# Sink attention in a two-block model: other banks for the second rotation, a new order on three engines, and an earlier fetch of the distance table

## What is computed

```python
def banded_sink_attention(q, k, v, sinks):
    logits = jnp.einsum('bnqhgd,bnkhd->bnhgqk', qb, kw) * (dh ** -0.5)
    logits = jnp.where(valid, logits, -jnp.inf)  
    m = jnp.maximum(jnp.max(logits, axis=-1), sink)
    probs = jnp.exp(logits - m[..., None])
    denom = jnp.sum(probs, axis=-1) + jnp.exp(sink - m)
    return jnp.einsum('bnhgqk,bnkhd->bnqhgd', probs, vw) / denom[..., None]

def swa_sink_mixer(h, positions, w_qkv, q_norm, k_norm, sinks, w_out):
    q, k, v = jnp.split(h @ w_qkv, [1024, 1280], axis=-1)
    q = apply_rope_2(rms_norm_2(q, q_norm), cos, sin)
    k = apply_rope_2(rms_norm_2(k, k_norm), cos, sin)
    return banded_sink_attention(q, k, v, sinks) @ w_out
```

## Time and profile before

| | |
|---|---|
| median of 3 runs | 2091.65 us (2090.82 to 2091.75) |
| the profiled execution: its own time | 2096.21 us |
| its span, first to last instruction | 2094.3 us |
| granted TensorE clock, mean over the span | 0.995 |
| PE / DVE / ACT / POOL busy | 99% / 85% / 67% / 3% |
| bytes moved, mean rate | 565.92 MB, 270 GB/s |

### The profile page before, as it was taken

The page is one execution under the profiler, slowest core; times in us unless marked ns, Lnnn a source line. Parts: engine busy times, 40 slices in busy tenths (PEclk is TensorE's granted clock), DMA queues, the critical chain, the costliest instruction groups (busy, mean ns, idle before and its releaser), DMA issues. The chain is left out here.

```text
span 2094.3 us, 27806 instructions
## 1 busy us (share of the span) xinstructions
PE 2067.1 (99%) x10830; PEld 1740.9 (83%) x10830; DVE 1779.1 (85%) x2358; ACT 1400.0 (67%) x1855; POOL 59.6 (3%) x58
## 2 busy tenths in 40 slices
PE   9999999999999999999999999999999999999999
PEld 8878888878888888888888888879988888778887
DVE  6776768789999999999999999988878888788887
ACT  5654547568888888888888888867745446565544
POOL 0011002001000000000000000000000000000000
PEclk9999999999999999999999999999999999999999
DMA  9537764659999999999999999954446555346552
GB/s 312 181 121 271 233 209 151 219 199 395 394 395 395 395 395 383 385 380 386 371 393 374 388 372 378 394 202 141 144 159 227 196 181 149 81 154 222 183 197 102
DMA packets 291275, 565.92 MB, mean 270 GB/s; under 512 B 13596, under 2 KB 120224, under 8 KB 290896
## 3 DMA queue, kind: packets, MB, share of 16 engines
q1 hardware_dynamic: 284480, 537.13, 71.8%
q0 software_dynamic: 5792, 23.78, 3.1%
q10 hardware_dynamic: 864, 3.15, 0.4%
HBM read 555.10 MB, written 12.59 MB: 271 GB/s over the span
## 5 line engine op out<-in xcount | busy, mean ns | idle before, releaser
L505 DVE TENSOR_TENSOR wl<-raw,wh 128x1024 fp32r<-128x1024 f32 x626 | 756.2, 1242 | 99.9 <-ACT wh L497 95.5
L497 ACT ACTIVATE wh<-raw 128x1024 fp32r<-128x1024 f32 x626 | 640.9, 1053 | 154.1 <-PE psum L542 61.7
L505 DVE TENSOR_TENSOR wl<-arena,wh 128x1024 fp32r<-128x1024 f32 x384 | 456.7, 1222 | 37.6 <-ACT wh L497 32.6
L497 ACT ACTIVATE wh<-arena 128x1024 fp32r<-128x1024 f32 x384 | 403.9, 1062 | 84.7 <-PE psum L542 82.5
L540 PE MATMUL psum<-wh,xhl 128*128 128x512 f32 (+1 forms) x1136 | 449.5, 396 | 1.8 <-DVE wl L505 0.9
L542 PE MATMUL psum<-wh,xhl 128*128 128x512 f32 (+1 forms) x1136 | 441.5, 389 | 0.0
L541 PE MATMUL psum<-wl,xhl 128*128 128x512 f32 (+1 forms) x1136 | 440.6, 388 | 0.0
L532 PE MATMUL psum<-xhl,wh 128*128 128x512 f32 x980 | 349.4, 396 | 0.0
L540 PE MATMUL psum<-wh,yh 128*128 128x512 f32 x752 | 295.6, 393 | 1.0 <-DVE yl L1714 1.0
L542 PE MATMUL psum<-wh,yl 128*128 128x512 f32 x752 | 293.0, 390 | 0.0
L541 PE MATMUL psum<-wl,yh 128*128 128x512 f32 x752 | 292.6, 389 | 0.0
(11 more groups left out here) (455 smaller groups left out, 2078.1 us busy)
## 6 DMA issues: line engine op xcount, KB each, us to landing
arena<-in_moe_g SPq DMA_DIRECT2D x72, 1024.0 KB, 8.8
arena<-in_moe_u SPq DMA_DIRECT2D x72, 1024.0 KB, 8.5
raw<-in_moe_d SPq DMA_DIRECT2D x64, 1024.0 KB, 8.8
arena<-in_moe_d SPq DMA_DIRECT2D x48, 1024.0 KB, 8.3
raw<-in_ff_up SPq DMA_DIRECT2D x48, 1024.0 KB, 5.2
raw<-in_moe_g SPq DMA_DIRECT2D x40, 1024.0 KB, 8.1
raw<-in_moe_u SPq DMA_DIRECT2D x40, 1024.0 KB, 9.2
raw<-in_ff_down SPq DMA_DIRECT2D x24, 1024.0 KB, 5.4
```

Of the source, the lines that this page charges most:

```text
L497: A.activation(unit_made(s, i)[0], raw_half(s, i), ACT.Copy).then_inc(*s.w_hi.tick(i))
L505: V.tensor_tensor(lo, raw_half(s, i), hi.bitcast(F), SUB).then_inc(*s.w_lo.tick(i))
```

## The change

It does five things:

- the rotation of the second half of the queries goes to banks 2 and 3 in place of 0 and 4;
- on PE `turned(3)` comes ahead of `sums(1)`;
- on DVE the masks of pieces 4 and 6 come ahead of the scales, `rows(0, 1)` too; the maxima of 4 and 6 come in a row, those of 5 and 7 share their three small steps; `rows(1, 0)` and the low parts of U+16 and U+17 move;
- on ACT `newer(5)` comes ahead of `soft(4)` and `newer(7)` ahead of `soft(6)`, and the high parts of some units come later;
- at the beginning the `hold_clock` after the first chunk has 2 matmuls in place of 3, and POOL fetches the distance table without waiting for x.

```diff
-                    hold_clock(7, 3, STILL[:, 0:P], STILL)
+                    hold_clock(7, 2, STILL[:, 0:P], STILL)
...
-    Q_BANKS, RO_BANKS, SS_BANK = {2: (0,), 0: (2, 3), 1: (0, 4)}, {2: (6,), 0: (6, 7), 1: (0, 4)}, {2: 4, 0: 4, 1: 1}
+    Q_BANKS, RO_BANKS, SS_BANK = {2: (0,), 0: (2, 3), 1: (0, 4)}, {2: (6,), 0: (6, 7), 1: (2, 3)}, {2: 4, 0: 4, 1: 1}
...
         logits(4, 6)
+        turned(3)
         sums(1)
-        turned(3)
         weigh(0, 1)
...
         turned(1)
+        turned(3)
         hi_to(main, U + 15)
-        turned(3)
-        hi_to(main, U + 16)
         weighed(0, 1)
         hi_to(main, U + 17)
+        newer(5)
         soft(4)
-        newer(5)
+        newer(7)
+        soft(6)
         hi_to(main, U + 18)
-        soft(6)
-        newer(7)
-        hi_to(main, U + 19)
         soft(5)
         turned(4)
         turned(6)
-        hi_to(main, U + 20)
+        hi_to(main, U + 19)
         soft(7)
         weighed(1, 0)
-        hi_to(main, U + 21)
+        hi_to(main, U + 20)
         turned(5)
         turned(7)
...
-        def maxima(u):
+        def maxima(*us):
...
+            for n, u in enumerate(us):
+                V.wait_ge(*dve.of(f"wi.l{u}"))
+                V.tensor_reduce(x[:, n, :], WE[u % 4], AX, MAX, negate=True).then_inc(*dve.tick())
...
         normal(3)
+        part_older(1)
         rows(0, 0)
-        part_older(1)
+        masked(4)
         part_older(3)
+        masked(6)
+        rows(0, 1)
         scales(1)
-        rows(0, 1)
+        maxima(4)
+        maxima(6)
         lo_to(main, U + 14)
-        begin(4)
+        older(5)
         lo_to(main, U + 15)
-        begin(6)
-        begin(5)
+        older(7)
+        maxima(5, 7)
         lo_to(main, U + 16)
         normal(4, 6)
-        begin(7)
+        lo_to(main, U + 17)
+        normal(5)
+        rows(1, 0)
         lo_to(main, U + 18)
-        normal(5)
         normal(7)
-        rows(1, 0)
...
-        G.wait_ge(*x_in[0].of("all"))
         G.dma_start(CT[0:32, o:o + n], d["consts"][0:32, o:o + n]).then_inc(*distances_in.tick())
```

More of the change, by code:

```diff
@@ L3223, in older, with soft_pair @@
                                   heads(bk(b), 2)[:, :, 0:P]).then_inc(*dve.tick(f"wi.l{u}"))
-        def maxima(u):
-            nm, _, sk, x = soft_cols(u)
-            gr, t, L = u // 2, u % 2, WE[u % 4]
-            _, r, _, _ = win_scales(gr // 2)
-            r4 = r[:, 8 * t:8 * t + 8].rearrange("p (j g) -> p g j", g=2)[:, gr % 2, :]
-            V.wait_ge(*dve.of(f"wi.l{u}"))
-            V.tensor_reduce(x, L, AX, MAX, negate=True).then_inc(*dve.tick())
+        def soft_pair(*us):
+            a = 64 + 16 * us[0]
+            return (SC[:, a:a + 64].rearrange("p (u n j) -> p u n j", u=2, j=4)[:, 0:len(us), n, :] for n in range(4))
+        def maxima(*us):
+            t, gr = us[0] % 2, us[0] // 2
+            _, r, _, _ = win_scales(gr // 2)
+            r4 = r[:, 8 * t:8 * t + 8].rearrange("p (j g) -> p g j", g=2)[:, gr % 2:gr % 2 + len(us), :]
+            ns = NSK[:, 4 * gr:4 * gr + 4 * len(us)].rearrange("p (u j) -> p u j", j=4)
+            nm, _, sk, x = soft_pair(*us)
+            for n, u in enumerate(us):
+                V.wait_ge(*dve.of(f"wi.l{u}"))
+                V.tensor_reduce(x[:, n, :], WE[u % 4], AX, MAX, negate=True).then_inc(*dve.tick())
             V.wait_ge(*dve.last())
@@ L3234, in maxima @@
             V.wait_ge(*dve.last())
-            V.tensor_tensor(nm, x, NSK[:, 4 * gr:4 * gr + 4], MIN).then_inc(*dve.tick())
+            V.tensor_tensor(nm, x, ns, MIN).then_inc(*dve.tick())
             V.wait_ge(*dve.last())
-            V.tensor_tensor(sk, nm, NSK[:, 4 * gr:4 * gr + 4], SUB).then_inc(*dve.tick(f"wi.m{u}"))
+            V.tensor_tensor(sk, nm, ns, SUB).then_inc(*dve.tick(*[f"wi.m{u}" for u in us]))
         def begin(u):
```

## The result

The changed kernel takes 2100.18 us, median of 12 runs (2095.71 to 2104.39). The kernel before, run beside it on the same chip, takes 2093.05 us, also 12 runs (2090.52 to 2097.20). The ratio is 1.0031 with an interval of 1.0020 to 1.0042. The change costs 7.1 us, where I had forecast 2.1. It is slower by 0.3% (the interval begins at 0.2%), and outside my range, also when the range is counted from this 2093.05 in place of the 2091.65 of three runs that I started from: it then ends 5.85 us above before.

The account below looks back on a forecast made before the run. PE was taken as the bound, busy 2067.1 of 2094.3 us. From 2091.65 us, -2.7 (beginning) + 1.6 (attention lists) + 3.2 (clock falls) = +2.1 gave 2093.7 us, range 2087.5 to 2097.5.

Parts of the forecast that it names:

- The lists: Sink attention: new engine orders worked against each other; projection 5.8 us earlier, then new PE waits, feed-forward part 1.6 us later.
- Rival 1: Sink attention: PE keeps the 5.8 us of the earlier projection, 2083.1 us; chance 0.13, another 0.05 for half of it.
- I take two falls, behind the two waits nearest to 3.48: +3.2 us: Sink attention: two of four new PE waits bring half clock, up to 1.6 us each; between 0 and 6.4 us.
- rival 2: Sink attention: the clock falls behind each of the four new waits, 4 x 1.6 us, giving 2097.0 us; chance 0.14.
- the beginning's bound: Kernel start: the small end of the beginning's gain, -1.5 us, if the clock falls there all the same.
- The term of the beginning, -2.7 us: Kernel start: earlier table fetch -1.5, half clock gone -1.6, one `hold_clock` matmul less -0.1, taken back +0.4 and +0.1 us.
- Rival 3: Kernel start: the beginning gives nothing, through a held-up first chunk or a clock falling anyway; 2096.5 us, chance 0.08.
- its first reason: Kernel start: the distance table's early fetch holds up the first chunk.
- the 0.1 us that I had put down for the table: Kernel start: the table's 48.5 KB now move beside the first chunk at 348 GB/s, costing some 0.1 us.

Follow-up runs that it names:

- e4: The whole change, with PE's four new waits in the attention filled by matmuls nobody reads: 2093.94 us, ratio 1.0002 to the kernel before.
- e6: e5 with four matmuls nobody reads added in PE's wait for the rotated queries, ahead of `logits(4, 6)`: 2086.59 us, ratio 0.9967 to before.
- e2: The changed kernel with the two edits of the beginning undone: 2098.58 us, ratio 1.0033 to the kernel before.
- e3: The kernel before with only the second half's rotation moved to banks 2 and 3, all lists as before: 2091.11 us, ratio 0.9990.
- e7: The kernel before with 7 matmuls nobody reads in PE's old 3.48 us wait ahead of the second rotation: 2092.62 us, ratio 0.9997.
- e8: e4 with `scales(1)` back ahead of `rows(0, 1)` on DVE and no filling behind `logits(5)`: 2091.89 us, ratio 0.9993 to before.
- e9: e8 with `normal(7)` ahead of `rows(1, 0)` on DVE and no filling ahead of `turned(7)`: 2091.06 us, ratio 0.9986 to before.
- e10: e9 with pieces 5 and 7 in their old places on ACT and DVE, filling only ahead of `logits(4, 6)`: 2086.76 us, ratio 0.9970 to before.
- e5: The kernel before with the start edits, rotation in banks 2 and 3, and `turned(3)` ahead of `sums(1)`; old DVE and ACT lists: 2089.90 us, ratio 0.9981.
- e1: The kernel before with the two edits of the beginning alone: 2092.47 us, ratio 0.9993.

## Why the prediction was wrong, point by point

**The lists were right.** Each wait came where it was put: ahead of `logits(4, 6)` 1.83 us (2.0 said), behind `logits(5)` for the low part 2.56 (2.8), ahead of `turned(4)` 2.86 (3.1), ahead of `turned(7)` 3.07 (3.3). The projection's start gained 5.9 us (5.8). With no fall in the stage it is 55.76 - 54.47 = 1.3 us longer (e4 against before); 1.6 was said. Rival 1, that the gain of 5.8 us stays, is refuted by the same rows. It does come true, and more, once the lists of DVE and ACT are the old ones and the first wait is filled: e6 has 48.16 us, 6.3 less than before.

**The step that failed** is "I take two falls, behind the two waits nearest to 3.48: +3.2 us". In the profiled execution it is exact: two falls, and the stage is 58.91 - 55.76 = 3.15 us longer than with the waits filled. But the forecast is for the median of many runs, and there the falls cost 6.2 us, the price I gave to rival 2 (6.4) with a chance of 0.14. The mechanism differs from rival 2's in its form, as far as the mean clocks and the profiled e2 tell (no run of the changed kernel's own lower group was profiled): not each wait with one fall of 1.6 us, but half of the runs with few falls, and half with many or long ones, as e2's 10 us in one piece, 20 us in all, worth 63.78 - 55.76 = 8.0 us of the stage. So the mis-sized thing was the cost of one fall: my 1.6 us is half of the 3.3 us at the beginning, where the same rows show 6.8 us in the stage itself, behind a wait followed by light work. The Trainium skill (TensorE: Matmul & The Clock Gate, Part 1) says that the gate does not start anew with a kernel, and that the number of slow matmuls at its start varies from run to run. The runs agree and show it in mid-kernel too: 2095.7 to 2104.4 us for one program at clocks of 0.997 to 0.992, and 2092.4 to 2096.0 with the waits filled. I had kept both ends of the range for this reason, and then put the middle where one execution would lie. Two slips of the working changed nothing in the sum: with the clock falling all the same the beginning's bound is -2.7 + 1.6 = -1.1 and not -1.5, and by my own terms the change costs more than it gives from the first fall on (-1.1 + 1.6 = +0.5), not from the third.

**The term of the beginning, -2.7 us, was mis-sized.** Alone it measured -0.6 by the medians and -1.5 by the ratio (-3.3 to +0.4 by the interval, so 2.7 is not excluded by that run alone); with it undone the rest of the change costs as much as all of it (1.0033 and 1.0031). In the profiled pair it is there in full: the matmuls of L1127 start at 34.9 before and at 31.9 after. But that execution before was an unlucky one: the other three with the old beginning start them at 32.7 (e2), 32.1 (e3) and 32.0 (e7), since the table landed sooner and the clock did not fall. The eight with the new beginning start them at 31.3 to 32.2, 31.7 in the mean. So old and new are 0.6 us apart in the mean, 1.2 with the execution before counted. Rival 3, that the beginning gives nothing, is near in size, though its first reason is not borne out: no hold-up of the first chunk can be told. ACT's first copy waits for that chunk, and starts at 3.55 to 3.73 us in the four executions with the old beginning and at 3.56 to 3.76 in the eight with the new one; the 0.1 us that I had put down for the table beside that chunk is below this scatter.

**The sum with the measured terms**: -0.6 for the beginning, +1.5 for the lists (e4 is 0.9 above before, and the beginning's 0.6 is in it), +6.2 for the clock: +7.1 us. The three add up by construction, since e4 is subtracted in one and added in the other. The +1.5 and the +6.2 hang on the same runs of e4; the stage's 1.3 is an independent reading of the first, and the 6.7 us of lost clock of the second. e2 is the check from outside: 1.5 + 6.2 = 7.7 us without the beginning, where it measured 5.5 by the medians and 6.9 by the ratio. So these terms are good to a us or two.

**Where the gain of the banks went** can be told part by part from the stages without half clock. From e6 to e4 are 7.6 us: the scales behind `rows(0, 1)` cost 2.3 (e4 to e8), `normal(7)` behind `rows(1, 0)` costs 1.0 (e8 to e9), the odd pieces ahead of `normal(4, 6)` cost 3.1 (e9 to e10, on DVE and ACT together). The last 1.2 us, e10 to e6, are the masks ahead of the scales and the units' places, and were not taken apart.

**What stays open.** Why the clock doesn't fall at all in one execution (after, behind the wait of 1.83 us) and falls for 10 us in another (e2, behind the same wait) was seen and not explained. How many of the 6.2 us come from the first wait alone wasn't tried on the changed kernel; e4 fills all four at once.

## What to carry to other kernels

On an engine that works its list in order, a wait costs what stands behind it: all three orders that lost time here put a step that waits for PE (`rows`, `older`) ahead of one that PE waits for (`scales`, `normal`). On a PE that is 99% busy, a wait of 2 us can be followed by more half clock than it is long, so a wait that cannot be removed is worth filling with matmuls: four of them were worth 3.3 us from e5 to e6. Look at the next wait too, since in e7 the fall only moved there and nothing clear was gained (filling both wasn't tried on that kernel). And price no term of a few us from one execution: read it in several, and look at the mean clock of every run before believing the profile's pair.

## What was not expected of the hardware

- The clock falls behind waits much shorter than 3.48 us: 1.82 us in e3, 1.24 us in e7. In both, narrow matmuls follow (64 rows, 128x2); the fall comes during the first of them in e3 and at their end in e7. That they play a part was not tested. In the other direction, waits of 1.83 and 3.07 us after the change were followed by no fall in the profiled execution.
- The falls of this stage lasted about 3.4, 6.8 or 10.2 us, by the execution.
- The same work falls or doesn't by the execution. Near 443 us, far from every edit, where all kernels here have the same instructions, the profiled executions after, of e1, e2, e6, e7 and e9 show half clock for about 3 us; before, e3, e4, e5, e8 and e10 show none. That is 6 of 12, whatever the kernel. Near 1400 and 1465 us all twelve are at half clock, each time for 3.4 or 6.8 us; these and the last microseconds are what is left in e4.
- The unchanged kernel spreads over 7 us in 34 runs, in step with its mean clock (2090.45 us at 0.998, 2097.40 at 0.993).
- The 0.5 KB of the table took 3.6 to 4.9 us when issued at 2.0 us (8 executions) and 5.2 to 6.7 when issued at about 5.2 (4 executions), before being the slowest of them.
